# Turning and routing the token tiles ahead of the first norm

## The reference

```
mix = hybrid_mixer(x, w_in, w_out, rel_bias)          # two attentions, one output projection
h   = layer_norm(ALPHA * x + mix, ln1_g, ln1_b)
# mixture of experts on h:
g_logits = h @ w_group + b_group                      # 4 groups, the best one is taken
e_logits = h @ w_expert[g] + b_expert[g]              # 8 experts in the group, the best two are taken
y   = gates of the two experts * (silu(h @ w_gate) * (h @ w_up)) @ w_down
out = layer_norm(ALPHA * h + y, ln2_g, ln2_b)
```

## Time and profile before

| | |
|---|---|
| times, three runs | 588.68, 588.72, 587.34 us (median 588.68) |
| the profiled execution | 588.45 us |
| its span | 586.7 us |
| busy PE, weight loads, DVE, ACT, POOL | 86%, 57%, 45%, 27%, 26% of the span |
| from the last output product to the first gate product | 282.2 to 321.7 us |

### The profile page before, as it was taken

One profiled execution on the slowest core, in us unless ns is written; L12 is line 12 of the kernel. 1 busy time (PEld: TensorE's weight loads), 2 busy tenths in 40 slices (PEclk: granted clock), 3 DMA queues, 4 the chain that ended last, 5 costly groups with the idle time before them and its releaser, 6 DMA issues.

```text
span 586.7 us, 7929 instructions
## 1 busy us (share of the span) xinstructions
PE 502.6 (86%) x3060; PEld 334.7 (57%) x3060; DVE 266.9 (45%) x434; ACT 159.4 (27%) x312; POOL 150.3 (26%) x129
## 2 busy tenths in 40 slices
PE   4999899999999996899832799999987779697790
PEld 4888676776667664688731455555545444454430
DVE  3300276797756555200761276453442314236167
ACT  4221354545455443122520011111110101111222
POOL 4434354455322211143001023222111102121000
PEclk9999999999999997799965899999999979899996
DMA  6432312951121116089984488999999999999663
GB/s 251 144 101 79 107 37 65 367 120 36 37 73 37 56 53 250 1 310 363 349 341 177 161 339 333 416 418 414 414 415 416 418 416 415 417 416 416 250 253 143
DMA packets 53239, 144.12 MB, mean 246 GB/s; under 512 B 11014, under 2 KB 27414, under 8 KB 45008
## 3 DMA queue, kind: packets, MB, share of 16 engines
q1 hardware_dynamic: 48160, 134.40, 59.8%
q0 software_dynamic: 5040, 9.18, 4.3%
HBM read 135.45 MB, written 16.27 MB: 259 GB/s over the span
## 4 chain that ended last, share of the span: by engine, by line
PE 37%; DMA 10%; DVE 6%; issue 4%; SPq 1%; POOLq 0%; DVEq 0%
PE bank L1424 16%; DMA gate_w<-in_w_gate 9%; PE bank L1451 7%; PE bank L1412 2%; PE bank L1220 2%; PE bank L1221 2%; PE bank L1222 2%; DMA xe<-h_rows,idx_all 2%; PE bank L1368 1%; PE bank L1437 1%; PE bank L1426 1%; DVE hx L1182 1%; DVE hx L902 1%; PE bank L1528 1%; SPq L368 0%
## 5 line engine op out<-in xcount | busy, mean ns | idle before, releaser
L1424 PE MATMUL bank<-gate_w,xeT 128*64 128x256 f32 x512 | 125.8, 402 | 27.7 <-issue 25.0
L1426 PE MATMUL bank<-up_w,xeT 128*64 128x256 f32 x512 | 126.2, 403 | 0.0
L494 POOL TENSOR_TENSOR w_lo<-raw,w_hi 128x1024 fp32r<-128x1024 f32 x32 | 80.6, 2520 | 130.5 <-ACT w_hi L608 130.4
L1424 PEld LDWEIGHTS bank<-gate_w,xeT 128*64 128x64 f32 x512 | 71.5, 145 | 62.3 <-issue 36.2
L1426 PEld LDWEIGHTS bank<-up_w,xeT 128*64 128x64 f32 x512 | 71.5, 145 | 0.0
L1046 DVE TENSOR_TENSOR silu_hid<-silu_hid,bank 64x256 f32<-64x256 f32 x32 | 13.5, 423 | 111.4 <-ACT silu_hid L732 110.7
L1451 PE MATMUL bank<-down_w,hidT 128*64 128x512 f32 x256 | 61.3, 598 | 0.9 <-issue 0.9
L732 ACT ACTIVATE silu_hid<-bank 64x256 f32<-64x256 f32 x32 | 12.0, 375 | 158.7 <-PE bank L1426 158.7
L1220 PE MATMUL bank<-xT_hi,w_hi 128*128 128x512 f32 x128 | 53.6, 418 | 0.8 <-ACT values L627 0.8
L608 ACT ACTIVATE w_hi<-raw 128x1024 fp32r<-128x1024 f32 x32 | 33.8, 1057 | 62.1 <-PE bank L1222 47.8
L1222 PE MATMUL bank<-xT_lo,w_hi 128*128 128x512 f32 x128 | 50.7, 396 | 0.0
(11 more groups left out here) (166 smaller groups left out, 793.4 us busy)
## 6 DMA issues: line engine op xcount, KB each, us to landing
gate_w<-in_w_gate SPq DMA_DIRECT2D x32, 1024.0 KB, 25.3
up_w<-in_w_up SPq DMA_DIRECT2D x32, 1024.0 KB, 24.7
down_w<-in_w_down SPq DMA_DIRECT2D x32, 1024.0 KB, 23.5
raw<-in_w_in SPq DMA_DIRECT2D x24, 512.0 KB, 3.9
expert_rows<-xe SPq DMA_DIRECT2D x1, 4096.0 KB, 15.1
raw<-in_w_out SPq DMA_DIRECT2D x8, 512.0 KB, 3.5
hx<-in_x SPq DMA_DIRECT2D x4, 512.0 KB, 4.9
h_rows<-hx SPq DMA_DIRECT2D x4, 512.0 KB, 11.4
```

Of the source, the lines that this page charges most:

```text
L494: nc.gpsimd.tensor_tensor(w_lo[:, slot, :], raw[:, slot, :], w_hi[:, slot, :].bitcast(F32), ALU.subtract).then_inc(s_lo, 1)
L1424: nc.tensor.matmul(GATE[h], xeT[:, m % 2, c, half(h)], gate_w[r][:, c, :], start=(c == 0), stop=(c == KD - 1))
L1426: mm = nc.tensor.matmul(UP[h], xeT[:, m % 2, c, half(h)], up_w[r][:, c, :], start=(c == 0), stop=(c == KD - 1))
```

## The change

TensorE turns the tiles as soon as the residual is there, ahead of the norm, and routes the raw rows. The norm enters on the logits: each tile's 36 columns are multiplied by `rstd`, and `nmean * rstd` (new: `offset`) times the column sums of `w_gained` is added. For that the reduction over `shifted_w` gets a second one over `w_gained` beside it (`dots`), and the dot product on TensorE is twice as wide. DVE normalises a tile behind its copy of the turned tile, in place, instead of between the residuals. The logits of tile t stand in bank 2t and no longer side by side in bank 0. Instead of one addition for all logits there are four preset operations (bias and mean's part, ahead of the routes' end) and four that take in the product. The lists of ScalarE, GpSimd and SP are not edited.

```diff
-        shift_dot = at("shift_dot", [P, G + E], F32, top[0] + 128)
+        dots = at("dots", [P, 2, G + E], F32, top[0] + 128)
...
+        offset = sb("offset", [P, T])
...
-            nc.vector.tensor_reduce(shift_dot[:, :], shifted_w[:, :, :].rearrange("p c n -> p n c"), AX.X, ALU.add
-                                    ).then_inc(s_gained, 1)
+            for n, w in enumerate((shifted_w, w_gained)):
+                ins = nc.vector.tensor_reduce(dots[:, n, :], w[:, :, :].rearrange("p c n -> p n c"), AX.X, ALU.add)
+            ins.then_inc(s_gained, 1)
...
                 mean(t)
-                if t >= 2:
-                    normalised(t - 2)
...
-            normalised(T - 2)
-            half_hT(0)
-            normalised(T - 1)
-            for t in range(1, T):
+            for t in range(T):
                 half_hT(t)
+                normalised(t)
...
+            nc.vector.tensor_tensor(offset[:, :], nmean[:, 0:T], rstd[:, 0:T], ALU.mult).then_inc(s_broute, 1)
             dve.wait_ge(s_dot, 2)
             nc.vector.tensor_tensor(b_route[:, :], b_route[:, :], bank[:, 1, 0:G + E], ALU.add
                                     ).then_inc(s_broute, 1)
-            dve.wait_ge(s_broute, 1)
-            dve.wait_ge(s_logit, T)
-            LG = bank[:, 0, 0:T * (G + E)].rearrange("p (t n) -> p t n", t=T)
-            then(nc.vector.tensor_tensor(logit[:, :, :], LG, b_route[:, :].unsqueeze(1).broadcast_to([P, T, G + E]),
-                                         ALU.add))
+            dve.wait_ge(s_broute, 2)
+            for t in range(T):
+                ins = nc.vector.scalar_tensor_tensor(out=logit[:, t, :], in0=bank[:, 1, G + E:2 * (G + E)],
+                                                     scalar=offset[:, t:t + 1], in1=b_route[:, :], op0=ALU.mult,
+                                                     op1=ALU.add)
+            ins.then_inc(s_broute, 1)
+            dve.wait_ge(s_broute, 3)
+            for t in range(T):
+                dve.wait_ge(s_logit, t + 1)
+                ins = nc.vector.scalar_tensor_tensor(out=logit[:, t, :], in0=bank[:, 2 * t, 0:G + E],
+                                                     scalar=rstd[:, t:t + 1], in1=logit[:, t, :], op0=ALU.mult,
+                                                     op1=ALU.add)
+            then(ins)
...
             def turn_h(t):
-                pe.wait_ge(s_h, t + 1)
+                pe.wait_ge(s_res, t + 1)
...
-                    mm = nc.tensor.matmul(bank[:, 0, t * (G + E):(t + 1) * (G + E)], hT[:, c, t * P:(t + 1) * P],
+                    mm = nc.tensor.matmul(bank[:, 2 * t, 0:G + E], hT[:, c, t * P:(t + 1) * P],
...
-                    nc.tensor.matmul(bank[:, 1, 0:G + E], ones_f[:, 0:1].to_broadcast([P, P]), shift_dot[:, :], start=True,
-                                     stop=True).then_inc(s_dot, 1)
+                    nc.tensor.matmul(bank[:, 1, 0:2 * (G + E)], ones_f[:, 0:1].to_broadcast([P, P]),
+                                     dots[:, :, :].rearrange("p n k -> p (n k)"), start=True, stop=True).then_inc(s_dot, 1)
```

## The result

The kernel after took 594.62 us (median of 4 executions, 593.92 to 597.03), the kernel before 588.70 beside it. The ratio is 1.0108, 95% interval 1.0086 to 1.0131: slower by 5.9 us, above the top of the range. Medians are taken over all executions, but the ratios leave out those more than 1.5% above the fastest of their kernel: among 60 executions of the kernel before, in this and the later sets, that is seven of 596.2 to 597.9 us and one of 1251.86. The profiled execution of the kernel after took 597.03, the slowest of its four, with a span of 595.3.

The account below looks back on a forecast made before the run. Bound by the chain from last row tile through routing and gather to the first gate matmul, which moves the weight stream. Gains 1.28 and 0.13 make 1.41; less 0.2 to 0.25 for clock, 1.2: 588.45 to 587.2 us, range 585.7 to 589.7.

Parts of the forecast that it names:

- a rival to which I gave 0.12: Between turns and routes: TensorE idles behind turn 1, the clock falls by 287.5; 589.0 to 594.9 us, taken 592; chance 0.12.
- ScalarE holds route 0, gain 1.28: Start of route 0: ScalarE's squares delay its first copy, so route 0 starts at 286.17 instead of 287.45, gain 1.28 us.
- DVE tail, 0.13: DVE's logit operations behind the routes: done with TensorE's last route; the last operation takes 0.18 instead of 0.31, gain 0.13 us.
- Stores and expert 5 late, cost 0: SP's queue: h stores and expert 5's weights issued 5.5 us later, hidden by transfer backlog; cost 0, at most 5.5 us.
- The clock, loss of 0.2 to 0.25: TensorE's first gate matmuls: work moved ahead by 1.4 us runs partly at half clock, taking 0.2 to 0.25 us off.
- the likeliest case: Whole kernel: the forecast itself, gain 1.2 us, 587.2 us with own range 586.4 to 587.9; chance 0.61.
- The end follows the first gate product about one for one: From the first gate matmul at 321.66 to the end: a microsecond gained before it moves the end about one microsecond.

Follow-up runs that it names:

- a1_wide: Kernel after with six 512-column products between the dot and route 0, in TensorE's gap behind turn 1: 587.51 us, ratio 0.9992 to the kernel before.
- c4_warm_before: Kernel before with groups of 11, 2, 16, 4 and 5 added 256-column products in TensorE's waits behind the routes: 588.56 us, ratio 0.9991.
- b1_gap: Kernel before with one added wait: the dot and route 0 wait for the fourth normalised tile: 594.63 us, ratio 1.0116.
- a3_act: Kernel after with ScalarE's copies of tiles 0 and 1 ahead of the fourth square: 584.51 us, ratio 0.9932; repeated at 584.63 us.
- c6_warm_fit: a3_act with 11, 2, 9, 6, 4 and 5 added 256-column products in TensorE's waits behind the routes: 580.85 us, ratio 0.9866 to the kernel before.
- a4_late: Kernel after with turns 0 and 1 held until the fourth residual is there: 587.79 us, ratio 0.9989 to the kernel before.
- c2_warm_before: Kernel before with groups of 22, 5, 40, 9 and 10 added 256-column products in TensorE's waits behind the routes: 598.62 us, ratio 1.0171.
- c1_warm: a3_act with groups of 22, 5, 40, 9 and 10 added 256-column products in TensorE's waits behind the routes: 600.16 us, ratio 1.0207 to the kernel before.
- c7_warm_late: a3_act with 8, 4 and 5 added 256-column products in TensorE's waits, only from the gather on: 583.12 us, ratio 0.9913 to the kernel before.
- c3_warm_act: a3_act with groups of 11, 2, 16, 4 and 5 added 256-column products in TensorE's waits behind the routes: 586.01 us, ratio 0.9955 to the kernel before.

## Why the prediction was wrong

The sum was right up to route 0, and the result was decided by a rival to which I gave 0.12.

- *ScalarE holds route 0, gain 1.28.* Right: 9.12 - 7.94 = 1.18, or 1.34 from the start of the route in the earlier trace rows, which the forecast used. The first copy ran from 7.31 us behind the first residual (285.98), forecast 285.52 - 278.17 = 7.35.
- *DVE tail, 0.13.* Right in the sum: from route 0 to gmax a1_wide takes 9.42, the kernel before 9.52. The last operation took 0.26, not 0.18; DVE was done with all before it and waited 0.32 us for the last route, so its tail held nothing up.
- *Stores and expert 5 late, cost 0.* Right as far as the runs go: in a1_wide expert 5's last matrix is issued 5.3 us later (forecast 5.5), and it gathers 1.28 earlier than before. The backlog hid the delay as forecast: from the issue of expert 4 on the DMA engines stay at a share near 1 until about 27.3 us behind the first residual in both kernels (305.5 before, 304.5 in a1_wide). The gather then takes 9.53 in a1_wide instead of 9.10, so 0.43 may be due to the queue; over all kernels in whose chain it stands it took 8.27 to 9.78, with no order in it that these runs show.
- *The clock, loss of 0.2 to 0.25.* This is the step that failed, and with it the choice of the likeliest case. The routes ran at half clock, which cost 24.73 - 17.36 = 7.37 us to gmax, against a1_wide. The rival had the place (behind turn 1), the moment (by 287.5; it was 287.3) and the price (7.6 if all of the work left is hit). It went wrong in its chance and in taking 592, in the middle, for its time. The argument against it was that the gaps of 1.0 and 0.36 us in the kernel before had cost nothing. That was read from one execution, and c4_warm_before shows an execution in which the first of these gaps did lose the clock. The change puts the two turns together and then has 1.34 us of nothing and a route; b1_gap shows that 0.9 us more of gap in that place, in the kernel before, was all it took. The row in favour of the rival, the clock falling 0.6 us behind 3.36 us of route products, was the one to follow. What exactly lets the clock fall stays open; the runs show which fillings and orders kept it.
- *Smaller part of the same step.* Even with the clock held through the routes, the 1.28 us at gmax are 0.85 at the first gate product and 0.26 at the last scaled tile (a1_wide). Of this, 0.43 is the gather, and the remaining 0.6 agrees with the 0.7 that I had named as the price if the later rise of the clock does not move with the work; this is one trace each, and the repeat of a3_act differs by up to 0.26. So the change without its loss of clock, as a1_wide stands for it, is worth 0.3 us by the traces and 0.5 by the ratio, not the forecast 1.2, and its interval (0.9977 to 1.0007) includes no change at all.
- *The end follows the first gate product about one for one.* The first gate product is 6.01 us late, the last scaled tile 6.42; the rest of this slowest execution added 1.7 and lies inside the scatter of the rest. Which part of that scatter is the transfers and which the clock is open.

## What to carry to other kernels

Before work is moved off TensorE's path, look at what TensorE will do in the time that becomes free: a gap of 1.3 us ahead of thin products cost 7.4 us, six times what the earlier start brought. When an engine's wait is removed, look for the next producer in line (here ScalarE's copies behind squares that nobody awaited) and reorder it in the same edit: a3_act gains 4 us with the change, and the change alone loses 6. Added wide products in TensorE's waits paid for themselves in c6_warm_fit, but only when sized from a row of the same shape and with the pause around the branch counted in. And one profile of a kernel is one execution: look at the spread of its times before a clock in it is called safe.

## What the runs showed of the hardware

- Filling the gap with 1.47 us of 36-column products did not keep the clock, 1.6 us of 512-column products of one instruction each did, at the same place and in the same kernel.
- 128x128 transposes directly in front of the routes kept it (a4_late), behind 1.41 us of waiting.
- An f32 product of 256 columns with 128 stationary columns takes 0.44 us in two instructions of 0.22 at full clock (80 in 17.54 us, c2_warm_before). The 16 products of one expert's gate and up, with 64 stationary columns each, go in 16 pairs of instructions, one every 0.215 us (338.56 to 341.58 in the kernel before), so 0.22 us for a product, because a gate and an up instruction run side by side.
- With the order of work of the kernel before, one profiled execution lost the clock in a gap of 1.02 us between two turns (c4_warm_before, at 285.3), while the profiled execution of the kernel before kept it through the same gap.
- Around the branch on a register TensorE paused for 2.49 us (c1_warm), 2.92 (c7_warm_late), 3.18 (c2_warm_before), 4.13 (c4_warm_before) and 5.25 (c3_warm_act) with nothing to wait for that the profile shows. The cause is open.
